# Expert rows of a two-layer diffusion block: from row pairs to single rows, with the plan's early allowance counted once

## The reference, cut to what matters

```python
def peer(h, wq, keys, u, v):
    q = (xs @ wq).reshape(PEER_BLOCK, PEER_HEADS, 2, PEER_HALF)
    ...                                     # scores of two key sets, top 16 of each
    top, j = lax.top_k(cand, PEER_TOPK)     # top 16 of the 256 sums
    eid = jnp.take_along_axis(cid, j, axis=-1)
    g = jax.nn.softmax(top, axis=-1)
    a = jax.nn.gelu(jnp.einsum('nd,nhjd->nhj', xs, u[eid]), approximate=False)
    return jnp.einsum('nhj,nhjd->nd', g * a, v[eid])
```

## Time and profile before

| | us |
|---|---|
| median of 3 runs (3432.03 to 3439.66) | 3435.36 |
| the profiled execution's own time | 3441.62 |
| its span in the trace | 3439.5 |
| busy: PE / DVE / ACT / POOL | 2810.3 / 1919.4 / 1111.6 / 853.5 |
| DMA moved 1071.76 MB, mean | 312 GB/s |

### The profile page before, as it was taken

The page is one execution under the profiler, slowest core; times in us unless marked ns, Lnnn a source line. Parts: engine busy times, 40 slices in busy tenths (PEclk is TensorE's granted clock), DMA queues, the critical chain, the costliest instruction groups (busy, mean ns, idle before and its releaser), DMA issues.

```text
span 3439.5 us, 40717 instructions
## 1 busy us (share of the span) xinstructions
PE 2810.3 (82%) x15162; PEld 1750.6 (51%) x15162; DVE 1919.4 (56%) x4582; ACT 1111.6 (32%) x3213; POOL 853.5 (25%) x772
## 2 busy tenths in 40 slices
PE   8999998989888999888775555699999986655555
PEld 6777887655545666564431111278788841211111
DVE  4564764566676556456676766422300256666665
ACT  2232002343574455323533232232310123323222
POOL 0000001234332333223344444200000034444443
PEclk9999999999999999999898776899999987776776
DMA  8264764989998999879999999733144299999998
GB/s 327 99 208 148 289 239 169 369 339 373 373 358 329 417 421 420 336 299 371 404 372 420 415 412 412 308 111 110 57 152 151 73 376 414 411 419 403 411 415 335
DMA packets 151780, 1071.76 MB, mean 312 GB/s; under 512 B 16668, under 2 KB 19356, under 8 KB 23200
## 3 DMA queue, kind: packets, MB, share of 16 engines
q0 software_dynamic: 110592, 805.36, 57.8%
q1 hardware_dynamic: 40992, 263.82, 20.5%
HBM read 1068.06 MB, written 1.05 MB: 311 GB/s over the span
## 4 chain that ended last, share of the span: by engine, by line
PE 51%; DMA 26%; DVE 12%; ACT 6%; issue 3%; POOL 2%; SPq 0%; DVEq 0%; POOLq 0%; ACTq 0%
PE bank L438 38%; DMA ring<-in_experts,eid 25%; PE bank L452 11%; DVE ring L1494 5%; POOL ring L1968 2%; ACT topk_work L1007 1%; ACT topk_work L1000 1%; DMA ring<-in_quads 1%; ACT topk_work L997 1%; ACT L997 1%; DVE state L1729 1%; PE bank L465 1%; PE bank L687 0%; DVE topk_work L1464 0%; PE bank L568 0%
## 5 line engine op out<-in xcount | busy, mean ns | idle before, releaser
L1968 POOL DMA_INDIRECT ring<-in_experts,eid x768 | 853.3, 1111 | 2563.2 <-PE bank L452 1284.2
L452 PE MATMUL bank<-ring,topk_work 64*64 64x512 f32 x6144 | 975.0, 763 | 557.6 <-ACT topk_work L1007 544.3
L1494 DVE CUSTOM_DVE_ANT_0 ring<-ring,h2tok 128x1024 f32<-128x1024 f32 x768 | 937.4, 1225 | 589.1 <-DMA ring<-in_experts,eid 574.9
L452 PEld LDWEIGHTS bank<-ring,topk_work 64*64 64x64 f32 x6144 | 234.7, 158 | 1185.5 <-ACT topk_work L1007 878.3
L997 ACT ACTIVATE topk_work<-topk_work 128x2 f32<-128x2 f32 x384 | 78.0, 203 | 1139.9 <-DVE topk_work L1494 1132.6
L438 PE MATMUL bank<-h_even,weights 128*128 128x256 f32 (+1 forms) x1280 | 293.2, 388 | 4.4 <-ACT h_even L1080 4.0
L438 PEld LDWEIGHTS bank<-h_even,weights 128*128 128x128 f32 (+1 forms) x1280 | 240.9, 190 | 60.8 <-issue 22.8
L438 PE MATMUL bank<-h_odd,weights 128*128 128x256 f32 (+1 forms) x1008 | 228.3, 382 | 0.0
L1007 ACT ACTIVATE topk_work<-const,topk_work 128x64 f32<-128x64 f32 x768 | 225.6, 341 | 0.2 <-ACT topk_work L1000 0.2
L438 PEld LDWEIGHTS bank<-h_odd,weights 128*128 128x128 f32 (+1 forms) x1008 | 187.5, 189 | 49.9 <-issue 23.8
L1000 ACT ACTIVATE topk_work<-topk_work 128x1 f32<-128x1 f32 x768 | 184.6, 287 | 12.6
(11 more groups left out here) (252 smaller groups left out, 3243.6 us busy)
## 6 DMA issues: line engine op xcount, KB each, us to landing
weights<-in_quads SPq DMA_DIRECT2D x151, 1024.0 KB
ring<-in_quads SPq DMA_DIRECT2D x84, 1024.0 KB, 4.9
ring<-in_experts,eid POOLq DMA_INDIRECT x768
weights<-in_quads SPq DMA_DIRECT2D x6, 768.0 KB
ring<-in_quads SPq DMA_DIRECT2D x6, 768.0 KB, 4.5
weights<-in_quads SPq DMA_DIRECT2D x12, 256.0 KB
xT<-in_xT SPq DMA_DIRECT2D x2, 1024.0 KB, 11.7
out<-state SPq DMA_DIRECT2D x4, 256.0 KB, 5.3
```

What stands on the lines that cost most here:

```text
L452: x = nc.tensor.matmul(acc[g][out, :], diag[mine, J % 4, :], ring[mine, J % RING, D + h * 512:D + (h + 1) * 512], start=first, stop=J % TI ...
L1494: v.tensor_tensor_reduce(row, row, h2tok[:, u // UNITS % 2, :], 1.0, 0.0, ALU.mult, ALU.add, dots[:, u % 2, j:j + 1]).then_inc(S["dot_done ...
L1968: pool.indirect_dma_start(ring[:, J % RING, :], None, d["experts"], bass.IndirectOffsetOnAxis(eid[:, u % 2, j:j + 1], 0)).then_inc(gathere ...
```

## The change

Rows are handled one at a time on PE, ACT and DVE. `row_pair(n)` becomes `row(J)`, all counts of pairs become counts of rows, and the waits are for one row's dot and one freed diagonal. ACT issues a gelu for each row. In the plan `LAG` goes from 5.0 to 4.0, counted from the one row's own landing, and `breathe` fixes the moment up to which a row may be early before its loop starts, where it was taken anew from the moved `plan.now` in each round. The look-ahead of ACT goes from 2 pairs to 4 rows, that of DVE from 3 pairs to 6 rows (2 and 4 rows near a tile's start). Which matmuls are done, in which order rows follow each other, and the transfers are as before.

```diff
-PER_LOAD, LANDS, LAG = 2.5, 2.0, 5.0
+PER_LOAD, LANDS, LAG = 2.5, 2.0, 4.0
...
-TURN_FROM, TURN_EVERY, TURN_LAG = 24, 4, 2
+TURN_FROM, TURN_EVERY, TURN_LAG = 48, 8, 4
...
-            def row_pair(n):
-                for J in (2 * n, 2 * n + 1):
...
+            def row(J):
...
+                pe.wait_ge(S["diag_ready"], J + 1)
...
-            def emit(n):
-                landing = plan.row(2 * n + 1)
-                placed_now[n] = (len(job_log), landing)
-                plan.now = max(plan.now, landing + LAG) + 0.2
-                row_pair(n)
...
-                for J in (2 * n, 2 * n + 1):
-                    plan.now += 0.95
-                    if (J + RING) // GROUP_ROWS == J // GROUP_ROWS:
-                        plan.gather()
-                cur["next"] = n + 1
+            def emit(J):
+                landing = plan.row(J)
+                placed_now[J] = (len(job_log), landing)
+                plan.now = max(plan.now, landing + LAG) + 0.1
+                row(J)
...
+                plan.now += 0.95
+                if (J + RING) // GROUP_ROWS == J // GROUP_ROWS:
+                    plan.gather()
+                cur["next"] = J + 1
...
-                end = plan.now + hole
-                while cur["next"] < cur["limit"] and plan.row(2 * cur["next"] + 1) + LAG <= plan.now + hole / 2:
+                end, early = plan.now + hole, plan.now + hole / 2
+                while cur["next"] < cur["limit"] and plan.row(cur["next"]) + LAG <= max(plan.now, early):
                     emit(cur["next"])
...
-                act.wait_ge(S["dot_done"], J + 2)
-                nc.scalar.activation(gel[:, m:m + 2], dots[:, par, j:j + 2], ACT.Gelu).then_inc(S["act_gelu"], 1)
-                act.wait_ge(S["act_gelu"], 3 * n + 1)
-                for c in range(2):
-                    nc.scalar.activation(gelw[:, m + c:m + c + 1], gel[:, m + c:m + c + 1], ACT.Copy,
-                                         scale=wts[:, par, j + c:j + c + 1]).then_inc(S["act_gelu"], 1)
+                act.wait_ge(S["dot_done"], J + 1)
+                nc.scalar.activation(gel[:, m:m + 1], dots[:, par, j:j + 1], ACT.Gelu).then_inc(S["act_gelu"], 1)
+                act.wait_ge(S["act_gelu"], 2 * J + 1)
+                nc.scalar.activation(gelw[:, m:m + 1], gel[:, m:m + 1], ACT.Copy, scale=wts[:, par, j:j + 1]).then_inc(
+                    S["act_gelu"], 1)
                 if J >= 4:
 
-                    act.wait_ge(S["row_used"], J - 2)
...
+                    act.wait_ge(S["row_used"], J - 3)
+                act.wait_ge(S["act_gelu"], 2 * J + 2)
+                nc.scalar.activation(diag[:, J % 4, :], ident_blk, ACT.Copy, scale=gelw[:, m:m + 1]).then_inc(S["diag_ready"], 1)
...
-                    if placed[n][0] > now and not (placed[n][1] + DIAG_LAG <= when and reached(n, now, 2)):
+                    if placed[n][0] > now and not (placed[n][1] + DIAG_LAG <= when and reached(n, now, 4)):
...
-                    deep = 2 if n % TILE_PAIRS == 3 else 3
+                    deep = {1: 2, 7: 4}.get(n % TILE_ROWS, 6)
```

More of the change, by code:

```diff
@@ L438, in mm @@
                 return nc.tensor.matmul(out, lhsT, rhs, start=first, stop=last, **kw)
-            def row_pair(n):
-                for J in (2 * n, 2 * n + 1):
[L442 to L455, removed]
+            def row(J):
+                k, first = J // TILE_ROWS, J % TILE_ROWS == 0
+                if first and J:
+                    for g in range(2):
+                        pe.wait_ge(*at("evicted", "acc", k - 1, g))
+                pe.wait_ge(S["diag_ready"], J + 1)
+                for h in range(2):
+                    out = slice(h * BLK, (h + 1) * BLK)
+                    for g in range(2):
+                        mine = slice(g * BLK, (g + 1) * BLK)
+                        x = nc.tensor.matmul(acc[g][out, :], diag[mine, J % 4, :],
+                                             ring[mine, J % RING, D + h * 512:D + (h + 1) * 512],
+                                             start=first, stop=J % TILE_ROWS == TILE_ROWS - 1, skip_group_check=True)
+                x.then_inc(S["row_used"], 1)
             def tile_sum(k):
@@ L948, in _ @@
                     cur["pace"] = 0.0
-                    rows_until(first_pair(p.beside + 1))
+                    rows_until(first_row(p.beside + 1))
                     tile_sum(2 * p.beside + 1)
@@ L964, in _ @@
                 full(x, "turned", m)
-            rows_until(first_pair(GROUPS))
+            rows_until(first_row(GROUPS))
             token_sums(1)
@@ L1037, in rows_until @@
                     cur["next"] += 1
-                    row_pair(cur["next"] - 1)
+                    row(cur["next"] - 1)
             def rows_before(*key):
@@ L1482, in lead @@
                     choose(u, part)
[L1484 to L1504, removed]
@@ new lines, in row @@
+            def row(J):
+                u, j = divmod(J, PTOP)
+                if j == 0:
+                    for m in range(2):
+                        if u % UNITS == 0:
+                            dve.wait_ge(*at("evicted", "ht", u // UNITS // 2, u // UNITS % 2, m))
+                dve.wait_ge(gathered[J % RING], 16 * (J // RING + 1))
+                row = ring[:, J % RING, 0:D]
+                v.tensor_tensor_reduce(row, row, h2tok[:, u // UNITS % 2, :], 1.0, 0.0, ALU.mult, ALU.add,
+                                       dots[:, u % 2, j:j + 1]).then_inc(S["dot_done"], 1)
+                if u + 1 < GROUPS * 2 * UNITS and (u + 1) not in LEADS:
+                    if j < PTOP // 2:
+                        choose(u + 1, 2 * j)
+                        choose(u + 1, 2 * j + 1)
+                if J % TILE_ROWS == 1 and J // TILE_ROWS in (1, 2, 3):
+                    tile_out(J // TILE_ROWS - 1)
+                if J % TILE_ROWS == 7 and J // TILE_ROWS in (1, 2, 3):
+                    add_tile(J // TILE_ROWS - 1)
+                if J == 5 * TILE_ROWS + 1:
@@ L1505, in row_pair @@
                     last_sum(0)
-                if n == 5 * TILE_PAIRS + 7:
+                if J == 5 * TILE_ROWS + 15:
                     last_norm(0)
```

46 lines of the change are left out of this document (19 added, 27 removed).

## The result

| us | median | lowest to highest | runs |
|---|---|---|---|
| before | 3437.51 | 3432.03 to 3443.59 | 4 |
| after | 3490.75 | 3485.81 to 3495.45 | 4 |

The ratio is 1.0154, 95% interval 1.0131 to 1.0178: 53 us slower, above the range of 3340 to 3447. The profiled execution of after took 3489.3, its span is 3487.3.

What follows compares the result with a forecast made beforehand. DMA was taken to bound rows-only parts, PE pass 3, and both in turn the mixed parts. Terms -12 - 2 - 24 - 10 - 6 + 16 = -38 gave 3403.6 us profiled, 3397 median; range 3340 to 3447.

Steps and rivals of the forecast that it cites:

- Rows alone, -12: Rows-only stretches (1850 to 2200, 2840 to 3400): DMA rate rises from 413 and 412 towards 421 GB/s, -12 us.
- the tail, -2: Kernel's end: behind the last dot PE finds only the last row's half left instead of a pair, -2 us.
- TensorE's waits, -24: Beside passes 1 and 2: PE's waits for diagonals shrink as single rows are ready earlier, -24 us (ends -84, +56).
- ScalarE, 0: One gelu per row, 384 more, and extra table loads stay hidden under ACT's idle time, 0 us.
- Slow clock, -10: Beside passes 1 and 2: fewer matmuls at the lower clock after waits, -10 us (ends -25, +10).
- Early allowance, -6: Pass 1's queries: the chain of early pairs breaks, rows go beside the first two query blocks, -6 us (ends -9, 0).
- More batches, +16: Beside passes 1 and 2: 45 row batches more than 144 on PE, 0.36 us each, +16 us (ends 0, +76).
- Waits only move: Rival, passes 1 and 2: twos still used together, saved waits return at the next place; -4 us, 3431, chance 0.15.
- The slower rival: Rival, mixed parts: PE pays for 130 more batches, waits as they are; +27 us, 3462, chance 0.19.

Runs made afterwards that it cites:

- s_diag2: The changed kernel with DIAG_LAG 2.0 instead of 3.0, only ScalarE's order differing; 3442.66 us, ratio 1.0009.
- pairs_once: The changed kernel's single-row handling, rows placed in twos, LAG 5.0, allowance counted once at each place; 3420.86 us, ratio 0.9941.
- pairs_lag4: Rows handled singly but placed in twos, allowance taken anew in each round, LAG 4.0 instead of 5.0; 3439.96 us, ratio 1.0.
- s_lag5: The changed kernel with LAG 5.0 instead of 4.0 and nothing else; 3437.22 us, ratio 0.9992.
- s_lag5_each: The changed kernel with LAG 5.0 and the allowance taken anew in each round, rows still placed singly; 3482.23 us, ratio 1.0122.
- s_each: The changed kernel with the allowance taken anew in each round and nothing else; 3698.57 us, ratio 1.0743.
- s_lag5_diag2: The changed kernel with LAG 5.0 instead of 4.0 and DIAG_LAG 2.0 instead of 3.0; 3426.84 us, ratio 0.9958.
- pairs_once_d2: Rows handled singly, placed in twos, LAG 5.0, allowance counted once, DIAG_LAG 2.0 instead of 3.0; 3409.49 us, ratio 0.9912.

## Why the prediction was wrong, point by point

**Rows alone, -12, and the tail, -2: right together, placed wrong.** The rate went to 419, and the third group gave 13.3 with the tail. The second group gave nothing per row: 418.2 / 158 = 2.65 us before, 396.2 / 149 = 2.66 after. The tail gave a little more than said: the last row's 8 matmuls take 1.09 us together, 1.06 after its dot, where the earlier trace rows had 3.69 for a pair, so 2.6 us went and not 1.85:

```profile
3476.35 0.08 DVE L1485 DVE_READ_ACCUMULATOR2_ANT topk_work<- 128x1 f32 x1
...
3477.49 1.09 PE L449 MATMUL bank<-ring,topk_work 64*64 64x512 f32 x8 [0.43 <-ACT topk_work L1000]
```

**TensorE's waits, -24: the step that failed.** They grew by 22.5. I reasoned that the row is 1.5 us riper at its place (2.49 earlier than its pair, less 1.0 of `LAG`), as if TensorE's place were the only one. The row goes through ScalarE first, and ScalarE's place is worked out with `DIAG_LAG`, which I named in the account of the plan and left out of the sum. With `LAG` down and `DIAG_LAG` kept, its lead was halved, and the gelu slid behind exponentials and their table changes. s_diag2 shows it, with nothing else touched: 48 of 53 us.

**ScalarE, 0: the same mistake from the other side.** I counted the tables (at most 90 more; there are 6) and a delay of 1.3 us for each. Their number did no harm. What a gelu table at a bad place brings in attention is 3.8 to 5.6 us at one TensorE wait: beside it stand an exponential and either that one's own table or its wait, or both. Torn rows of the mixer and of gated attention wait up to 8.6 and 5.7 us. The Trainium skill (ScalarE: Activation LUTs, "What ACT_TABLE_LOAD costs") would have a drain of about 1.38 us in each. In the rows above the load begins 0.02 us after the instruction before it (231 of the 241 loads begin within 0.05) and the gelu 0.02 after the load: no drain stands there, so that isn't what is missing.

**Slow clock, -10: wrong sign; it went with the waits.** From the mixer to the tail of pass 2, length times (1 - granted clock) went from 64.8 to 104.0 us. In attention it is as large as the waits.

**Early allowance, -6: inside its ends, wrong cause.** The place went from 13.3 to 4.6. Of these 4.6, 4.03 are a wait of TensorE for ScalarE, of another kind:

```profile
1510.30 3.18 PE L888 MATMUL bank<-const,h_odd 128*128 128x128 f32 x8 [4.03 <-ACT h_odd L1072]
```

So 8.7 us went there, but the four rows are now done in the mixer and in attention. At the 1.72 us of a further row they cost some 7 there, so the net is an estimated -2. pairs_once keeps the 12.9 with the allowance counted once, and pairs_lag4 has 4.6 with it taken anew. So have s_lag5 and s_lag5_each, with `LAG` 5.0 and single rows. The rows went because `LAG` 4.0, or single placement, uses up the group earlier. What the once-counted allowance does is to hold single rows back from a runaway worth 208 us at `LAG` 4.0 (s_each) and 45 at 5.0; I had reasoned on pairs, in holes of 8 us, and never put single rows in.

**More batches, +16: right in number, and the price fits.** 144 became 194, inside 185 to 195. But only 85 of the 194 have 8 matmuls, where I had said most: 65 have 16 and 37 have 24, and a batch of two rows or more can be torn. In pool and merge, where little else changed, 17 batches more, 2 rows fewer and 5.7 us less of waits come to 371.3 us; by 0.36 a batch and 1.72 a row it would be 376.2 + 6.1 - 3.4 - 5.7 = 373.2, so this stage bears the price out within some 2 of 6 us.

**The rivals.** "Waits only move" is near what s_lag5 shows (3437) once the lead is back. The slower rival had the sign and one half of a sentence ("the smaller LAG sends rows to PE less ripe"), but its price was batches: 50 of them, 18 us. With the range resting on that price, its end of 3447 was too low.

Taken together, `LAG` 5.0 to 4.0 costs 17.6 us in pairs and 53.5 singly; placing singly costs 16 at `LAG` 5.0 (3420.86 to 3437.22) and 51 at 4.0 (3439.96 to 3490.75, where the allowance differs too); handling singly gains 18.

A rival for what single placement costs once the lead is back was left untested: the batches themselves. s_lag5 has 44 batches more than pairs_once between the mixer and the tail of pass 2 (191 and 147). At 0.36 us each that is 16 us, the whole distance. TensorE's waits ahead of rows are not longer there (109.5 us against 117.6); its busy time is, by 38 us: some 12 for seven rows more, 16 for the batches, and the rest goes with a lower clock (0.945 for 0.955). s_lag5_diag2 and pairs_once_d2 stand 17 us apart with the same 191 and 147. The same estimate, handling -18 and +0.36 for each batch above before's 144, puts s_lag5 1 us below before and s_diag2 level with it; measured are 3 below and 3 above. So late gelus, most of them in torn batches, explain the loss where the lead is 1 us; for the 16 us at a lead of 2, batches are as good an account as torn rows.

The runs set side by side here were on different chips, each beside before (3437.51 to 3440.33 there), so a difference of 2 us between them says nothing.

What stays open: of attention's 13 to 17 us between s_lag5 and the kernels with pairs, how much is torn rows and how much its one row more and its other grouping; and how the 16 us part between torn rows and batches. Rows placed singly on TensorE and yet never torn on ScalarE were not tried, nor what turned the runaway loose in the mixer at `LAG` 4.0 and not at 5.0.

## What to carry to other kernels

Where each engine's order is written out by a plan, a lag on one engine is a lead on another: list every constant that is compared with the one you change, and work out each engine's place before and after, not only that of the engine that waits. Handle work in small pieces if you like, but place them in few batches. Keep the pieces that one engine takes in one go together on the others as well, above all where the lead is short and a table change or an instruction with a wait of its own can come between. And try a rule such as an allowance on the new grain: it may be stable for pairs and run away for singles.

## What was not expected of the hardware

A wait of TensorE cost about twice its length in attention: 20 us more of waits came with some 21 us more at the lower clock, and the two rows behind the 5.62 us wait took 3.69 us where two take 1.95. In rows-only parts the clock fell (0.73 to 0.69) and TensorE's busy time rose (333.75 to 369.25 us in 560) while the rate went up, since there DMA sets the pace (its share is 1.01 in both) and a slow TensorE cost nothing.
